# Three landing buffers, seven weight slots and a last group of five chunks in a split-precision transformer kernel

## Time and profile before

| | us |
|---|---|
| median of 3 runs | 2729.57 |
| lowest and highest | 2729.12, 2731.09 |
| the profiled execution | 2729.38 |
| its span, first to last instruction | 2727.6 |
| TensorE (PE) busy | 2701.1 |
| VectorE (DVE) busy | 1939.7 |
| ScalarE (ACT) busy | 1541.6 |
| GpSimd (POOL) busy | 532.1 |
| granted TensorE clock | 0.999 |

### The profile page before, as it was taken

One profiled execution on the slowest core, in us unless ns is written; L12 is line 12 of the kernel. 1 busy time (PEld: TensorE's weight loads), 2 busy tenths in 40 slices (PEclk: granted clock), 3 DMA queues, 4 the chain that ended last, 5 costly groups with the idle time before them and its releaser, 6 DMA issues.

```text
span 2727.6 us, 34494 instructions
## 1 busy us (share of the span) xinstructions
PE 2701.1 (99%) x12754; PEld 2214.2 (81%) x12754; DVE 1939.7 (71%) x2831; ACT 1541.6 (57%) x2646; POOL 532.1 (20%) x930
## 2 busy tenths in 40 slices
PE   8999999999999999999999999999999999999998
PEld 7887788888888888886888888788788888888887
DVE  6877777777667777767786787778764765745764
ACT  6647764654766465457654655765454454444543
POOL 3211221221112122016221221222110021110120
PEclk9999999999999999999999999999999999999999
DMA  9967488687748868751786886578675586764773
GB/s 292 292 229 257 152 272 286 222 278 241 255 130 278 289 218 274 258 201 48 238 282 227 277 296 222 166 252 280 230 261 201 187 269 231 239 205 163 245 243 113
DMA packets 386919, 633.87 MB, mean 232 GB/s; under 512 B 25760, under 2 KB 255136, under 8 KB 386496
## 3 DMA queue, kind: packets, MB, share of 16 engines
q1 hardware_dynamic: 350752, 535.02, 59.2%
q0 software_dynamic: 35856, 96.30, 11.1%
q10 hardware_dynamic: 144, 0.36, 0.0%
HBM read 593.26 MB, written 38.32 MB: 232 GB/s over the span
## 4 chain that ended last, share of the span: by engine, by line
PE 96%; DVE 2%; ACT 1%; issue 0%; DMA 0%; SPq 0%; POOL 0%; DVEq 0%; ACTq 0%
PE ps L741 40%; PE ps L896 28%; PE ps L747 20%; PE ps L706 2%; PE ps L783 1%; PE ps L971 1%; PE ps L1002 1%; PE ps L863 1%; ACT SB L1696 1%; PE ps L1012 0%; ACT JUNK L1530 0%; PE ps L979 0%; DMA RAW<-in_ffn_w_in 0%; PE ps L813 0%; PE ps L1144 0%
## 5 line engine op out<-in xcount | busy, mean ns | idle before, releaser
L741 PE MATMUL ps<-HI,XH 128*128 128x512 f32 x2400 | 939.4, 391 | 1.9 <-DVE LO L1968 1.9
L741 PE MATMUL ps<-LO,XH 128*128 128x512 f32 x2400 | 934.3, 389 | 0.0
L1963 DVE TENSOR_TENSOR LO<-RAW,HI 128x1024 fp32r<-128x1024 f32 x468 | 563.3, 1219 | 320.6 <-ACT HI L1510 319.0
L1510 ACT ACTIVATE HI<-RAW 128x1024 fp32r<-128x1024 f32 x468 | 491.8, 1059 | 475.9 <-PE ps L896 284.0
L747 PE MATMUL ps<-HI,XL 128*128 128x512 f32 x2400 | 740.5, 390 | 0.3
L1968 DVE SCALAR_TENSOR_TENSOR LO<-RAW,GC,HI 128x512 fp32r<-128x512 f32 (+1 forms) x896 | 617.2, 742 | 140.0 <-ACT HI L1517 138.8
L1517 ACT ACTIVATE HI<-RAW,GC 128x512 fp32r<-128x512 f32 (+1 forms) x896 | 586.4, 714 | 202.8 <-PE ps L747 173.9
L741 PEld LDWEIGHTS ps<-HI,XH 128*128 128x128 f32 x2400 | 450.6, 188 | 99.2 <-DVE LO L1968 4.8
L747 PEld LDWEIGHTS ps<-HI,XL 128*128 128x128 f32 x2400 | 449.5, 188 | 98.6 <-DVE XL L2004 5.3
L741 PEld LDWEIGHTS ps<-LO,XH 128*128 128x128 f32 x2400 | 450.6, 188 | 92.0
L2693 POOL DMA_DIRECT2D AX<-turned x440 | 239.5, 551 | 368.7 <-DMA turned<-AT 307.6
(11 more groups left out here) (241 smaller groups left out, 2325.7 us busy)
## 6 DMA issues: line engine op xcount, KB each, us to landing
RAW<-in_ffn_w_in SPq DMA_DIRECT2D x350, 512.0 KB, 5.0
RAW<-in_ffn_w_out SPq DMA_DIRECT2D x88, 1024.0 KB, 6.3
RAW<-in_w_ada SPq DMA_DIRECT2D x48, 1024.0 KB, 6.2
RAW<-in_w_in SPq DMA_DIRECT2D x44, 1024.0 KB, 5.5
RAW<-in_w_ffn_in SPq DMA_DIRECT2D x88, 512.0 KB, 5.2
turned<-AT POOLq DMA_DIRECT2D x110, 256.0 KB, 2.7
AX<-turned POOLq DMA_DIRECT2D x440, 64.0 KB, 3.7
RAW<-in_diff_w_in SPq DMA_DIRECT2D x24, 1024.0 KB, 5.4
```

The costliest lines, as they stand in the source:

```text
L741: e.matmul(ps[:, b + t, 0:nw], XH[:, k, t * P:(t + 1) * P], q[s][:, c * nw:(c + 1) * nw], start=(k == 0 and q is HI), stop=False)
L1510: e.activation(HI[n % NSPLIT][:, 0:t.width], RAW[t.buf][:, h * t.width:(h + 1) * t.width], ACT.Copy).then_inc(s_hi, 1)
L1963: e.tensor_tensor(LO[n % NSPLIT][:, 0:w], RAW[t.buf][:, at[1] * w:(at[1] + 1) * w], HI[n % NSPLIT][:, 0:w].bitcast(F32), ALU.subtract).the ...
```

## The change

One landing buffer of 8 KB per partition less, one slot (4 KB of high and 4 KB of low parts) more, and the FFN stages' last group of w_out chunks has five chunks instead of four, the seventeen before it being single. `STAGE_END` moves by 8 KB, since the slots stand before the stage's own buffers and the landing buffers after them.

```diff
-NRAW = 4
+NRAW = 3
 HW = TW // 2
-NSPLIT = 6
+NSPLIT = 7
 
 SBUF_FROM, SBUF = 16512, 229344
-STAGE_END = 152 * 1024
+STAGE_END = 160 * 1024
...
                 rows_by(st.w0 + 4 * JP, lambda k, t: AH[:, k, t * P:(t + 1) * P],
-                        lambda k, t: AL[:, k, t * P:(t + 1) * P], FC, [1] * 18 + [4], ready, hook, s_end0,
+                        lambda k, t: AL[:, k, t * P:(t + 1) * P], FC, [1] * 17 + [5], ready, hook, s_end0,
                         by_halves(st), early_rows(st))
```

## The result

| | before | after |
|---|---|---|
| median of 5 runs, us | 2729.62 | 2742.12 |
| lowest and highest | 2729.12, 2731.09 | 2735.65, 2744.12 |
| profiled execution; its span | 2729.38; 2727.6 | 2735.65; 2733.9 |

After over before is 1.0041, 95% interval 1.0031 to 1.0052: slower by more than the 0.2% that a measurement of this kernel can tell. The median lies 3.1 us above 2739, the upper end of the predicted range, and 7.1 above that of the forecast's own, 2730 to 2735. Two things are to be explained: the loss, and that the runs after spread over 8.5 us where those of before spread over 2. The profiled execution after is the fastest of the five, so its trace shows the mildest case; a second profile stands under the first experiment.

A forecast was written before the change was run, and what follows sets the result against it. The prediction took TensorE to bound the kernel. From the profiled 2729.38 us it took 3.0 for the group of five and added 6.5 for three landing buffers, giving 2732.9 us, with a range of 2726.4 to 2739.

The forecast's parts named there:

- The bound: TensorE, busy 2701.1 us of 2727.6; the change wins or loses only TensorE's waiting, read from distances between starts.
- Part 1: Last group of five: row-0 chain starts 1.36 us earlier at FFN ends; gain 3.0 us, bounds 0.3 and 3.5.
- the hand-over: FFN to first mix2 stage: waits for row-0 result (0.62 us) and XL (0.16) end; gain 1.0, bounds 0.3 and 1.5.
- gone or under 0.3: Sign in the trace after: the wait at the first mix2 hand-over is gone or under 0.3 us.
- three ffn2 ends: Ends of ffn2 stages, said to show no wait, so no gain from the group of five there.
- Part 2: Seventh slot: wins nothing alone, lets a group of five keep the next stage's first two splits ready.
- Part 3: Three landing buffers: loads issued later, stalls at NSA and both mix2 starts; loss 6.5 us, bounds 0.8 and 13.
- NSA 1.1 and 1.6: NSA stage: 1.1 us stall at the second transposes, 1.6 us for the second window loads.
- Split 9: Mix2 starts: TensorE waits for split 9's low part, 1.5 us in the first stage and 2.3 in the second.
- the fifth tile: Weight tile of mix2 holding splits 8 and 9; in the first stage forecast to land at 1988.1, not before 1980.83.
- the rival that I gave 0.28: Late fifth tile costs more: mix2 +3, exchange for the scores +1, NSA +2, giving 2738.9 us; chance 0.28.
- The rule against the trace: Weight-load landing: skill formula estimates 4.4 us, no mix2 stall, 2729.1; trace shows 11.1 in mix2; forecast follows the trace.

The follow-up runs named there:

- the first experiment: The changed kernel run once more, unchanged, for a second profile (also called again): 2743.13 us, ratio 1.0048 to the kernel before.
- the pair of mended kernels: Changed kernel and kernel before, both with decay table, q/k copies, NSA's second window loads and first mix2 scores moved: 2726.19 and 2729.07 us.
- before_xl_first: Kernel before, with VectorE making the first XL between the two low parts at a folded boundary, not behind both: 2729.64 us, ratio 1.0002.
- group_of_five_alone: Kernel before with only the last group of five, keeping four landing buffers and six slots: 2762.55 us, ratio 1.0121.
- filled_wait: Changed kernel plus 12 useless 512-column matmuls ahead of TensorE's wait for the k block in each mix2 stage: 2739.0 us, ratio 1.0034.
- copy_before_split: Changed kernel, with ScalarE copying the exchanged q and k blocks ahead of the splits of mix2 blocks 2 and 3: 2741.16 us, ratio 1.0044.
- both_orders: copy_before_split, plus ScalarE and VectorE splitting up to 9 instead of 8 before mix2's block 0 is copied out and rotated: 2738.84 us, ratio 1.0035.
- three_buffers_alone: Kernel before with only three landing buffers, keeping six slots and a last group of four: 2742.93 us, ratio 1.0056.
- copies_between_splits: Changed kernel with only ScalarE's mix2 copies moved, q's ahead of split 16 and k's ahead of split 20: 2734.82 us, ratio 1.0018.

## Why the prediction was wrong

**The bound, and the way to read it: right.** Everything won or lost was distance between TensorE's starts.

**Part 1: right in mechanism and size at the boundaries, right in the sum with luck at the hand-over.** All seven boundaries lost their 0.29 and 0.05 more, the four attention ends kept theirs. The hand-over gave 0.8 where I had 1.0, but not as I said: the wait for the row-0 result did not go, a wait of 0.64 for ScalarE's XH copy took its place, against my sign of "gone or under 0.3". (I also wrote of three ffn2 ends; there are two ffn2 stages, and the second ends the kernel.) In all 3.0 was forecast, the traces give 3.2, and the pair of mended kernels shows 2.9 to 3.3. before_xl_first qualifies the reason: the earlier chain wins it, the order of low parts and XL alone wins nothing.

**Part 2: right as far as it went.** I said that the seventh slot alone wins nothing and serves to let a group of five live. What it prevents I then put at nothing, in the expectation of group_of_five_alone, and it is 33 us.

**Part 3, the places: right.** NSA 1.1 and 1.6 forecast, 0.9 and 1.35 seen (with restarts). Split 9: 1.5 and 2.3 forecast, 1.5 and 1.6 seen. That is 6.5 against 5.3, and the thirteen other stages lose nothing, as written.

**Part 3, what follows in mix2: the step that failed.** I followed the fifth tile up to the low part of split 9 and stopped there, as if the later tiles came as before. They do not: with three buffers full and VectorE rotating, no load goes out for 13.4 us and the DMA engines stand still for 4 of them, so the eighth to the eleventh tile are late as well, and the q and k copies stand behind the first splits of the ninth and the eleventh. The late q copy in turn holds back the k block's exchange. The sum had nothing for this; the rival that I gave 0.28 had "+1" for the exchange. It measured 2.7 + 1.1 in the mildest run and 3.7 + 5.8 in the second profile.

**The clock: missing from the sum.** In the two profiles of the changed kernel the waits of 2.5, 3.6 and 5.6 us were followed by half the clock, at 1.5 us for the first and 2.4 for the last. I priced a wait at its own length everywhere; these stretches show that this is wrong here, and filled_wait that they go when the wait is filled.

**The range** ended at a rival whose price was built from single rows. The term that I missed is also the one that varies, so the range was too narrow and on the wrong side of 0.2%: the late fifth tile costing more, at 0.28, had the right sign and the right stage, but only a small part of the mechanism.

**The rule against the trace.** The trace sided with the rows: the load took 11.1 us beside the table, and 5.2 without it. The second figure lies near the estimate of 4.4 by the Trainium skill (DMA: Bandwidth & Descriptors, Anatomy of one DMA), whose formula is given there for loads that GpSimd issues, while these are SP's. The Trainium skill (DMA: Bandwidth & Descriptors, Issuing engines are not separate DMA queues) says that loads of SP and GpSimd run on the same 16 engines and interleave. The experiment agrees: taking GpSimd's loads away made SP's land 5.9 us sooner.

## What to carry to other kernels

With one buffer less, do not stop at the first late load: list for each engine what stands behind *every* split that now waits, above all small copies on which another chain depends, and ask when the buffers are all full, since the queue then stands still and the backlog comes later. Move a small copy ahead of only the one instruction that is late; ahead of more, it holds up work that was ready. When a shorter ring is weighed, price a wait of TensorE of some microseconds with what it does at a lower clock afterwards, and look at more than one profile if the runs spread.

## What the runs showed of the hardware

- TensorE's granted clock was 0.50 behind waits of 2.5 us (after), 3.6 and 5.6 (again) and 3.4 and 3.3 (copy_before_split), and 1.00 behind those of 0.9 and 1.4 in after. A wait's length alone did not decide it. Behind the two waits of 3.4 in both_orders it was 1.00 once and 0.50 once; behind one of 2.0 in three_buffers_alone (near 2379 us) it was 0.50, and behind one of 2.1 in copies_between_splits 1.00. In group_of_five_alone it was 0.50 behind the waits of 1.9 us near 194 and 495 us and 1.00 behind those near 680 and 1168. Behind the same attention wait of 1.55 us near 280 it was 0.50 in the profile before and 1.00 in the one after. Why is open.
- A lowered stretch behind a wait cost 1.5 us (behind 2.5 us of waiting) and 2.4 (behind 5.6). Useless matmuls in the wait's place avoided it.
- The same load, with the same neighbours, landed 7.8 us after its issue in one execution and 13.0 in another.
- A 512 KB write of GpSimd held its read back for 8.05 us when it was issued 2.3 us behind a 1.5 MB load, and as long when it was issued together with a 1 MB load; in the changed kernel it was 3.10 us.
